# The attention passes of a hybrid decoder layer on Trainium2: four stages made one pipeline of 34 turns

## The reference, cut to what matters

```python
# three groups g of (window, dilation): (128, 1), (512, 4), (2048, 16); 4 heads x 128 each
qd = rope(rms_norm(dq[:, :, :, 0], dil_qn_g), pos)
kd = rope(rms_norm(dq[:, :, :, 1], dil_kn_g), pos)
for gi, (wd, r) in enumerate(DIL_GROUPS):
    # query t reads t - j*r, j = 0..wd/r; returns the output and the log of the denominator
    o, l = dilated_band(qi, ki, vi, r, wd // r)
# cross-attention, no positions
k = rms_norm(k.reshape(B, M, MEM_HEADS, MEM_HD), mem_kn_g)
qm = rms_norm(q_m.reshape(B, S, MEM_HEADS, MEM_HD), mem_qn_g)
sm = jnp.einsum('bshd,bmhd->bhsm', qm, mem_k) * (MEM_HD ** -0.5)
om = jnp.einsum('bhsm,bmhd->bshd', jax.nn.softmax(sm, axis=-1), mem_v)
```

## Time and profile before

| | us |
|---|---|
| median of 3 runs | 5937.02 (5933.73 to 5939.94) |
| profiled execution | 5942.84 |
| its span | 5941.2 |

### The profile page before, as it was taken

How to read it: one execution, slowest core, us unless ns; L and a number is a source line. 1 busy time by engine, 2 the same in 40 slices (tenths; PEclk the granted TensorE clock), 3 DMA queues, 4 the chain that set the end, 5 groups by cost and what they waited for, 6 DMA issues and landing times. The chain is left out here.

```text
span 5941.2 us, 55349 instructions
## 1 busy us (share of the span) xinstructions
PE 4848.2 (82%) x17762; PEld 3079.4 (52%) x17762; DVE 2600.4 (44%) x5524; ACT 1804.7 (30%) x4697; POOL 1595.2 (27%) x1401
## 2 busy tenths in 40 slices
PE   7999999956644448987996888888888888888898
PEld 6888888856544338983433333333333333333353
DVE  2111111146344432102224666666666666666664
ACT  3111111123223221102222444444444444444433
POOL 0000000025334301001002444444444434444433
PEclk9999999965566565558998999999999999999989
DMA  7989888711132322235216999999999999999988
GB/s 251 298 272 307 270 281 268 235 62 56 57 98 83 87 59 110 101 124 218 95 55 274 421 421 421 421 421 421 420 419 416 416 416 411 418 414 414 406 356 355
DMA packets 315418, 1640.60 MB, mean 276 GB/s; under 512 B 41240, under 2 KB 85912, under 8 KB 173272
## 3 DMA queue, kind: packets, MB, share of 16 engines
q0 software_dynamic: 167344, 1179.45, 48.7%
q1 hardware_dynamic: 112416, 236.91, 11.8%
q10 hardware_dynamic: 35456, 221.91, 11.5%
HBM read 1551.85 MB, written 315.93 MB: 314 GB/s over the span
## 5 line engine op out<-in xcount | busy, mean ns | idle before, releaser
L2385 PE MATMUL ex_ps_y<-ex_rows,ex_diag 128*128 128x512 f32 (+1 forms) x4224 | 2028.3, 613 | 402.1 <-ACT ex_diag L2181 383.4
L2307 DVE CUSTOM_DVE_ANT_0 ex_rows<-ex_rows,ex_n2u 128x1024 f32<-128x1024 f32 x1056 | 1294.5, 1226 | 940.8 <-DMA ex_rows<-scratch_uv,ex_E 931.0
L2133 POOL DMA_INDIRECT ex_rows<-scratch_uv,ex_E x1056 | 1157.8, 1096 | 1723.1 <-PE ex_ps_y L2385 1493.4
L2385 PEld LDWEIGHTS ex_ps_y<-ex_rows,ex_diag 128*128 128x128 f32 (+1 forms) x4224 | 729.2, 188 | 1604.0 <-ACT ex_diag L2181 939.7
L307 PE MATMUL pj_ps<-pj_w_hi,pj_nT 128*128 128x470 f32 (+1 forms) x3456 | 784.2, 378 | 22.1 <-PE pj_ps L307 14.0
L307 PEld LDWEIGHTS pj_ps<-pj_w_hi,pj_nT 128*128 128x128 f32 (+1 forms) x3456 | 622.1, 181 | 149.5 <-issue 32.0
L2169 ACT ACTIVATE ex_gel<-ex_dots 128x1 f32<-128x1 f32 x1056 | 213.8, 202 | 1366.2 <-DVE ex_dots L2307 1365.1
L211 DVE COPY pj_zo<-pj_ps 128x470 f32<-128x470 f32 (+1 forms) x108 | 69.7, 645 | 897.6 <-PE pj_ps L307 752.8
L2181 ACT ACTIVATE ex_diag<-ex_ident,ex_w 128x128 f32<-128x128 f32 x1024 | 411.0, 401 | 50.8 <-PE ex_ps_y L2385 17.9
L307 PE MATMUL pj_ps<-pj_w_lo,pj_nT 128*128 128x470 f32 (+1 forms) x1728 | 406.3, 377 | 0.0
L211 ACT COPY pj_zo<-pj_ps 128x470 f32<-128x470 f32 (+1 forms) x108 | 59.6, 552 | 996.8 <-PE pj_ps L307 622.7
(11 more groups left out here) (362 smaller groups left out, 4651.0 us busy)
## 6 DMA issues: line engine op xcount, KB each, us to landing
pj_w<-in_w_in POOLq DMA_DIRECT2D x24, 1880.0 KB, 14.2
scratch_z<-pj_zo SPq DMA_DIRECT2D x192, 235.0 KB, 8.7
scratch_uv<-in_peer_u ACTq DMA_DIRECT2D x8, 4096.0 KB, 21.2
scratch_uv<-in_peer_v ACTq DMA_DIRECT2D x8, 4096.0 KB, 38.9
scratch_uv<-in_peer_u ACTq DMA_DIRECT2D x4, 8192.0 KB, 37.7
scratch_uv<-in_peer_v ACTq DMA_DIRECT2D x4, 8192.0 KB, 69.0
out_dk_s<-in_cache_dil_k ACTq DMA_DIRECT2D x8, 4088.0 KB, 44.4
out_dv_s<-in_cache_dil_v ACTq DMA_DIRECT2D x8, 4088.0 KB, 56.3
```

Source lines behind the costliest of these rows:

```text
L2133: pool.indirect_dma_start(out=rows[:, p % SLOTS, :], out_offset=None, in_=d["uv"], in_offset=bass.IndirectOffsetOnAxis(ap=E[:, turn % 4, k ...
L2307: nc.vector.tensor_tensor_reduce(out=row, in0=row, in1=n2u[:, tile % 2], scale=1.0, scalar=0.0, op0=ALU.mult, op1=ALU.add, accum_out=dots[ ...
L2385: last = nc.tensor.matmul(y[0:n, 512 * c:512 * c + 512], diag[:, p % DIAGS, 0:n], rows[:, p % SLOTS, D + 512 * c:D + 512 * c + 512], start ...
```

## The change

`attend` is called four times as before, but the last three calls return at once and the first does all four passes: 34 turns, of which 0 to 23 are the three dilated groups, 24 and 25 the two key tiles of the memory, 26 to 33 the memory's queries. All is unrolled. The steps run from 0 to 39; in step n

- SP: x and table load of turn n+1, v load of n-4, output stores of n-5, k store of n-1
- POOL: `xr` and `t2` of n-1, `tg` of n
- ACT: squares of n, whole weights' copy of n-5, q and k copies of n-2, exponentials of n-4, roots of n
- DVE: mask and maximum of n-4, sums of n, `t1` of n-1, output and `lse` of n-5, `y` of n-1
- PE: weights' transposes of n-5, transposes of n-2, product with v of n-5, scores of n-3

Key turns have no scores. x, v and kT get three buffers, `qT`, `e`, the statistics and the softmax columns two; the memory's keys and values get tiles of their own. The three masks are loaded once and a turn takes a slice; a turn with one key tile leaves the other out. A class `Count` gives the value of a semaphore after a turn from the list of turns that count. The diff, cut to its core:

```diff
+class Count:
+    def __init__(self, sem, turns, per=1):
+        self.sem, self.turns, self.per = sem, turns, per
+    def upto(self, turn):
+        return self.per * sum(1 for u in self.turns if u <= turn)
 def attend(nc, d, group):
+    if group:
+        return
...
+    KEYS, ASK = NG * NT, NG * NT + MEM // P
+    N = ASK + NT
+    NX, NV = 3, 3
...
+        x, tab = sb("x", [P, NX, 2 * H, P]), sb("tab", [P, 2, 2, P])
+        tg = sb("tg", [P, 2, 2, P])
+        xr, t1, t2 = sb("xr", [P, 2 * H, P]), sb("t1", [P, 2 * H, P]), sb("t2", [P, 2 * H, P])
+        qT, kT, kTm = sb("qT", [P, 2, H, P]), sb("kT", [P, 3, H, P]), sb("kTm", [P, 2, H, P])
+        e, pT = sb("e", [P, 2, H, 2, P]), sb("pT", [P, H, 2, P])
...
+            def load_x(u):
+                after(sp, xr_done, u - NX)
+                after(sp, sq_done, u - NX)
...
+            for n in range(LAST + 1):
+                if 2 <= n + 1 < N:
+                    load_x(n + 1)
+                if at(n, 4) is not None and is_dil(n - 4):
+                    load_v(n - 4)
+                if asks(n, 5) is not None:
+                    store_o(n - 5)
+                if at(n, 1) is not None and not is_mem(n - 1):
+                    store_y(n - 1)
...
+            def scaled(u):
+                after(pool, rs_done, u)
+                after(pool, x_in[u % NX], u)
+                after(pool, t1_done, u - 1)
+                after(pool, y_done, u - 1)
...
+            def angles(u):
+                after(pool, tab_in[u % 2], u)
+                after(pool, t1_done, u - 1)
+                after(pool, t2_done, u - 1)
...
+            for n in range(LAST + 1):
+                if at(n, 1) is not None:
+                    scaled(n - 1)
+                    if is_dil(n - 1):
+                        crossed(n - 1)
+                if at(n, 0) is not None and is_dil(n):
+                    angles(n)
...
-                nc.scalar.copy(pT[:, 0:2, w], ps_p[:, 0:2, w]).then_inc(pT_act.sem, 1)
+            def turned_weights(u):
+                after(act, p_t, u)
+                after(act, o_done, u - 1)
+                nc.scalar.copy(pT[:, :, w], ps_p[:, :, w]).then_inc(pT_out.sem, 1)
...
+            for n in range(LAST + 1):
+                if at(n, 0) is not None:
+                    squares(n)
+                if asks(n, 5) is not None:
+                    turned_weights(n - 5)
+                if at(n, 2) is not None:
+                    turned(n - 2)
+                if asks(n, 4) is not None:
+                    powers(n - 4)
+                if at(n, 0) is not None:
+                    roots(n)
...
-                nc.vector.tensor_copy(pT[:, 2:4, w], ps_p[:, 2:4, w]).then_inc(pT_dve.sem, 1)
...
+            def rotated(u):
+                after(dve, t_done, u - 2)
+                after(dve, y_stored[u % 2], u - 2)
+                if is_dil(u):
+                    after(dve, t1_done, u)
+                    after(dve, t2_done, u)
+                    nc.vector.tensor_tensor(y[:, u % 2], t1[:], t2[:], ALU.add).then_inc(y_done.sem, 1)
...
+            for n in range(LAST + 1):
+                if asks(n, 4) is not None:
+                    masked(n - 4)
+                if at(n, 0) is not None:
+                    sums(n)
+                if at(n, 1) is not None and is_dil(n - 1):
+                    rotary(n - 1)
+                if asks(n, 5) is not None:
+                    output(n - 5)
+                if at(n, 1) is not None:
+                    rotated(n - 1)
...
+            for n in range(LAST + 1):
+                if asks(n, 5) is not None:
+                    turn_weights(n - 5)
+                if at(n, 2) is not None:
+                    turn(n - 2)
+                if asks(n, 5) is not None:
+                    values(n - 5)
+                if asks(n, 3) is not None:
+                    score(n - 3)
```

More of the change, by code:

```diff
@@ L986, in attend @@
[L986 to L992, removed]
@@ L998, in attend, with after @@
+        def after(eng, count, turn):
+            if count.upto(turn):
+                eng.wait_ge(count.sem, count.upto(turn))
         block = ctx.enter_context(nc.Block())
         z, zm = d["z"][0:SEQ, :], d["zm"]
[L1001 to L1018, removed]
+        N_CONSTS = 12
@@ L1020, in _, with at, asks @@
+        LAST = N + 5
+        def at(n, lag):
+            return n - lag if 0 <= n - lag < N else None
+        def asks(n, lag):
+            u = at(n, lag)
+            return u if u is not None and not is_key(u) else None
         @block.sync
         def _(sp):
[L1022 to L1034, removed]
@@ L1099, in _ @@
+            for i in range(2):
+                after(sp, y_stored[i], N)
+                after(sp, o_stored[i], N)
         @block.gpsimd
@@ L1183, in step @@
[L1183 to L1195 removed]
+                if is_dil(u):
+                    after(act, e_done, u)
+                    after(act, lse_done, u - 2)
+                    nc.scalar.activation(lnd[:, j], den[:, j], ACT.Ln).then_inc(lnd_done.sem, 1)
@@ L1344, in step, with turn_weights @@
-            def step(p, f, b):
-                if f:
-                    front(*f)
-                if b:
-                    back(*b)
-                    values(*b)
-            steps(pe, step)
+            pe.wait_ge(consts_in, 16 * N_CONSTS)
+            def turn_weights(u):
+                after(pe, e_done, u)
+                after(pe, pT_out, u - 1)
+                for h in range(H):
+                    for n in tiles(u):
+                        last = nc.tensor.transpose(ps_p[:, h, n, :], e[:, u % 2, h, n, :], ident[:])
+                last.then_inc(p_t.sem, 1)
@@ new lines, in score @@
+            def score(u):
+                after(pe, qT_out, u)
+                after(pe, kT_out, min(u, ASK))
+                after(pe, sm_done, u - 1)
+                for h in range(H):
+                    for n in tiles(u):
+                        key = kTm[:, n] if is_mem(u) else kT[:, (u - 1 + n) % 3]
+                        last = nc.tensor.matmul(ps_s[:, h, n, :], qT[:, u % 2, h, :], key[:, h, :], start=True, stop=True)
+                last.then_inc(scores.sem, 1)
+            for n in range(LAST + 1):
[7 more added lines that the diff above has]
+                    score(n - 3)
```

477 lines of the change are left out of this document (185 added, 292 removed).

## The result

The changed kernel takes **5683.97 us** (median of 4 runs, 5683.12 to 5684.46); the kernel before took 5935.38 us beside it. Ratio 0.9575, 95% interval 0.9559 to 0.9592: 251 us less. The profiled execution took 5683.68 us around a span of 5682.0 us.

What follows compares the result with a forecast made beforehand. No engine was full, so a serial chain per step was taken as the bound; 21.8, 198, 23, 46 and 15.5 gave a 304 us stage for 540.4, 236 less than 5937.0: 5701 us, range 5686 to 5745.

Steps and rivals of the forecast that it cites:

- Loop (a): DVE and POOL in a dilated step: `y`, rest of `tg`, xr, half products with t1, starts; 8.3 us.
- 23 x 8.6 = 198: Dilated turns: 23 more turns after the first `y`, to `y` of the last, at 8.6 us each, 198 us.
- the 0.3 on top: Dilated steps: 0.3 us added to 8.3 for x loads and SP's queue in the last eight turns, and the clock.
- 7 x 6.6 = 46: Memory pass: seven steps between the first and last mask, bound by PE, at 6.6 us each, 46 us.
- first `y`: Stage start to the first `y`: 20.1 us as before, with 3 more constants to issue 21.8.
- five steps: From the last dilated `y` to the first memory mask: three one-tile steps and two nearly empty ones, 23 us.
- the last turn: End of the memory pass: from the last turn's mask to the next stage as before, 15.5 us.
- The range: Whole kernel: 5686 to 5745 us; own range 8.3 to 9.0 us a dilated step, 5694 to 5711.
- Rival 1: PE's clock: transposes don't count as activity, so it falls in two-tile steps; 7 us more, 5708 us; chance 0.12.
- the 0.85 that I named: Attention stage: a granted PE clock above 0.85 was named as a sign that the prediction is right.
- Rival 2: Dilated steps: waits of in-order queues interlock, a step takes 10 us; 32 us more, 5733 us; chance 0.17.
- Rivals 3 to 5: Rms-to-`y` chain stays serial, 5754 us, chance 0.04; PE stays at 1.2 GHz, 5769, 0.05; x load closes one-step loop, 5962, 0.01.

Runs made afterwards that it cites:

- e5: Against the changed kernel, ACT copies the cosine half of `tg` from SBUF to PSUM and t1 reads it there: 5668.67 us.
- e4: Against the changed kernel, PE makes the weights' transposes twice, into the same place: 5688.68 us.
- e7: Against the changed kernel, ACT instead of DVE makes the negative maximum: 5685.50 us.
- e6: Against the changed kernel, `tg` of the first eight turns is stored and from turn 10 loaded instead of made again: 5679.64 us.
- e10: Changed kernel plus t1's cosines via PSUM, `tg` loaded from turn 10, negative maximum on ACT, memory scores ahead of values, v loaded a step earlier: 5664.88 us.
- e2: Against the changed kernel, passes fused with all new buffers, but each engine goes through its turns in the old order: 5871.34 us.

## Why the prediction was right or wrong

- **The mechanism held.** Loop (a) sets the dilated steps, whatever the number of tiles: shown by the waits, by e5 (1.0 us out of the loop, 1.0 out of the step), by e4 (0.9 us of PE's work added, nothing lost) and by e7 (0.6 us of DVE's time taken away, nothing won).
- **The term that failed is "23 x 8.6 = 198".** The rows gave 8.3 and the 0.3 on top were for x, SP and the clock. None of them cost anything: the squares waited for x 7.7 us in all between 1700 and 1885, and never with POOL waiting behind them, and where the clock fell PE's work filled its own idle time. And the loop closed in 8.20, since the starts between its parts came to 0.2: 188.7 us, 9.3 less.
- **"7 x 6.6 = 46"** measured 40.3, 5.7 less (distances of 3.9, 7.3 and five of 5.8). I added up 1.06, 0.65, 2.02 and 2.05 from the earlier trace rows and a wait. But groups that follow each other on PE overlap: above, values at 1739.88 with a duration of 1.95 are followed by the scores at 1741.67, 1.79 later. One of the five equal memory steps of the changed kernel:

```profile
1925.20 1.04 PE L1273 MATMUL at_ps_p<-at_ident,at_e 128*128 128x128 f32 x8
1926.08 0.60 PE L1281 MATMUL at_ps_t<-at_ident,at_y 128*128 128x128 f32 x4
1927.34 2.05 PE L1294 MATMUL at_ps_o<-at_vm,at_pT 128*128 128x128 f32 x16 [0.67 <-ACT at_pT L1177]
1929.23 1.95 PE L1304 MATMUL at_ps_s<-at_kTm,at_qT 128*128 128x128 f32 x16
1931.02 1.04 PE L1273 MATMUL at_ps_p<-at_ident,at_e 128*128 128x128 f32 x8
```

  From start to start that is 0.88, 1.26, 1.89 and 1.79, 5.82 together, where my sum was 6.4 and my term 6.6. The wait for ACT's copy, 0.67, was there as I had put it at 0.6; PE's own work was 5.15 and not 5.8, and the 0.2 on top cost nothing.
- **The other terms:** first `y` 19.7 for 21.8 (the three constants cost nothing that shows), five steps 21.9 for 23, the last turn 14.7 for 15.5. All five were too long, and that is why they add up instead of cancelling: 285.2 for 304.
- **The range.** Its low end took 8 us off for "cheaper key and end steps", but put 8.3 as the least for a dilated step, and nothing for PE's overlap. Each cushion was on the same side, and the lower end was made of the same cushions.
- **Rival 1** (transposes don't count): the transposes of `y` at 1738.95 took 1.09 and the values 1.95 in the steps shown, not 1.96 and 3.77. The clock did fall in other steps (the values at 1764.49 took 3.38) and averaged 0.82 in the stage, under the 0.85 that I named; it cost the dilated steps nothing, as their period shows. **Rival 2** (10 us steps by in-order queues) didn't come, but e6 and e10 show it at work as soon as loop (a) is shorter. **Rivals 3 to 5**: no step over 8.3, POOL not waiting for roots or x.
- **A reading that did no harm:** I took the half products for 2.57 us and t1's 1.23 in their 3.80. Without t1 beside them they took 2.78 in the kernel before too (at 1732.25), so t1 cost them 1.0; the sum of the loop has the 3.80 and is the same.
- What fusing and reordering are worth each I had not split: 104 and 151 us, or 65 and 190 the other way round (e2).

## What to carry to other kernels

Look for the loop that closes over one step and add up its rows, with what two engines cost each other when both work on operands in SBUF; then don't pad the sum with waits that lie on other loops. What is queued behind a wait on an in-order queue (here SP and DVE) is the next loop, and taking out the first one shows only what lies between them. For a chain of matmul groups on one engine, take distances of starts, not durations.

## What the runs showed of the hardware

- DVE's products and sums of two SBUF operands and POOL's products ran one after the other, the later one waiting: `tg` 2.32 behind `y` in the changed kernel, `y` 2.27 behind `tg` in e2. With one operand of DVE's in PSUM neither held up the other (1.22 beside 2.78, e5).
- A small operation was held up too: the negative maximum of 128x4 on DVE took 0.17 us before; in the changed kernel it took 0.59 where POOL's xr was running, and 0.78 on average over all 32. Reductions and the mask's operation beside the same product kept their 1.2 us. The Trainium skill, SBUF — State Buffer, section Who interferes with whom, has both: tensor_scalar may take the pair of ports that VectorE shares with GpSimd, a reduction never does, and the order of issue decides who blocks; these rows agree. I had read no price of this kind into the maximum, and e7 shows that it cost nothing.
- The clock did not fall in a step in which PE had only transposes and waiting for 4.5 us, 1741.65 to 1746.14 (e4): it was granted at 1.00 there.
